# A two-block transformer kernel: the feed-forward's up projection with its units on the partitions

## The chip, the cores and the metric

One core of a Trainium2 chip runs the whole program. The metric is the device time of one execution in microseconds. The kernel before takes 1305.74 us (median of 3 runs, 1304.75 to 1306.25). Engines: PE is TensorE, with PEld its loads of stationary operands; DVE is VectorE, ACT is ScalarE, POOL is GpSimd; SP issues most loads.

## What is computed

256 tokens with 1024 channels pass through a first block (a layer with three kinds of attention and a layer with dilated attention, each followed by a feed-forward) and a second block (feed-forward, a mixer of three branches, feed-forward). The change touches the four feed-forwards alone. They are all of this form, with 2816 hidden units:

```python
def rmsnorm(x, g):
    y = x32 * lax.rsqrt(jnp.mean(x32 * x32, axis=-1, keepdims=True) + RMS_EPS)
    return (y * g.astype(jnp.float32)).astype(x.dtype)

def swiglu(h, w_up, w_down):
    a, b = jnp.split(h @ w_up, 2, axis=-1)
    return (jax.nn.silu(a) * b) @ w_down

x = x + swiglu(rmsnorm(x, norm_ffn[layer]), ffn_w_up[layer], ffn_w_down[layer])
```

The second block adds half of the feed-forward's result.

## The kernel before

**Products in three parts.** Every float32 operand of a large product is split into an upper part, rounded to fp32r, and a lower part, the rest, also fp32r. A product is then upper x upper, upper x lower and lower x upper (`mm3`, L193 to 197). Weights arrive from memory in units of 128 x 2048 numbers, three slots in turn: SP loads a unit into `RAW`, ACT copies it to `WH` (`split_hi`), DVE writes the rest to `WL` (`split_lo`). `hi_done`, `lo_done` and `unit_used` count these.

**A feed-forward stage** (`ffn_sync`, `ffn_scalar`, `ffn_vector`, `ffn_tensor`, r = 0 to 3) takes the 2816 hidden units in 11 steps of 256. A step has an `up` of two weight units (each 4 of the 8 channel blocks, 256 gate columns and 256 value columns) and a `down` of one. In `up`, the tokens are the stationary operand: for each of 2 tiles of 128 tokens and each of 8 channel blocks, `mm3` makes three products of 512 columns (256 gate, 256 value) into the tile's bank, 48 in all. The tile's row scale (the rmsnorm's) is not in the operand; it goes in as the scale of the tanh (`RH`), silu(a) being a(1 + tanh(a/2))/2, and as a factor of the residual (`RF`). For each tile ACT makes the tanh from the bank (L579, L581), DVE two operations (L627, L630), and the gated rows `GG` have tokens on the partitions. PE turns them with four transposes (`turn`, L702) into bank 2, ACT copies the turned rows to `OTH` (L585), DVE writes the rest to `OTL` (L635), and these are the stationary operands of `down`: 24 products of 512 columns into banks 4 to 7, which add up over the 11 steps.

**Order of the work.** Each engine has a list written out by hand, synchronised by counting semaphores. PE: `up(0)`, then in each step `up(s + 2)`, `down(s + 1)`, `turn(s + 2)` (a hardware loop of 8 steps), and at the end `up(10)`, half of `down(9)`, `turn(10)`, the rest of `down(9)`, `down(10)`. In the third stage (r = 2), the memory rows of the mixer are transposed among these last parts (`norm_tensor`).

**The start of a stage.** The stage's input rows are turned tile by tile: `tile_tensor` (L400) has 8 transposes per tile, ACT makes the upper parts (L409), DVE the lower ones (L457, `tile_lo`, counted one by one). Tile 1 is turned in the middle of `up(0)`. `tile_vector` places the split of the second unit between tile 1's fourth and fifth lower part. With `first=True`, `up_half` takes tile 0's upper rows first (L204), its lower rows (L211), turns tile 1, and does the same for it; then comes the second unit, tile by tile (L195 to 197).

## Time and profile before

| | |
|---|---|
| median of 3 runs | 1305.74 us (1304.75 to 1306.25) |
| the profiled execution | 1304.92 us, span from first to last instruction 1303.1 us |
| PE busy | 1270.1 us, 97% |
| PEld busy | 1059.4 us, 81% |
| DVE busy | 811.3 us, 62% |
| ACT busy | 644.9 us, 49% |
| POOL busy | 271.3 us, 21% |
| mean granted clock of PE | 0.996 |
| one transpose of 128 columns (L400), its own length | 272 ns |
| one load of a 128x128 fp32r operand | 188 ns |

The page gives busy time by engine, a strip of 40 slices, the chain of waits that ended last, and groups of instructions. PE is at nine tenths or more in nearly every slice. A product's own duration is longer than the distance to the next one, since they are pipelined; the distances have to be read from start times in the timeline. Times in the rows count from the start of the span.

### The profile page before, as it was taken

To read this page: it belongs to the slowest core of one execution; us is meant where nothing else is said; L and a number is where in the kernel's file an instruction comes from. 1 tells how busy PE (TensorE), PEld (TensorE's weight loads), DVE (VectorE), ACT (ScalarE), POOL (GpSimd) and SP (SyncE) were. 2 spreads that over 40 slices of the span, in tenths; PEclk is the share of its full clock that TensorE was granted. 3 is DMA by queue.
4 is the path that set the end of the run, shared out by engine and by line. 5 is a ranking of instruction groups with operands and counts; after the bars stand their busy time and mean duration, and the time that the engine had idled before them with its cause. 6 is when DMAs were issued, how large, how long until landed. Compare 5 with 4: busy or idle time off the path is not lost.

```text
span 1303.1 us, 19302 instructions
## 1 busy us (share of the span) xinstructions
PE 1270.1 (97%) x7279; PEld 1059.4 (81%) x7279; DVE 811.3 (62%) x1210; ACT 644.9 (49%) x946; POOL 271.3 (21%) x362
## 2 busy tenths in 40 slices
PE   6999999999999999999999999999999999999997
PEld 5986788888799977888888788888887778888886
DVE  3468675555574486654555755556789877755554
ACT  4438654444453366543444655445444683544442
POOL 6420210000000041102000489701186210200000
PEclk9999999999999999999999999999999999999999
DMA  9970556555455644467655465654544436556651
GB/s 288 273 136 19 166 173 193 182 184 186 159 194 180 177 115 130 161 195 175 228 183 179 167 194 186 220 188 147 194 130 146 146 121 202 181 190 193 191 188 41
DMA packets 155883, 224.77 MB, mean 172 GB/s; under 512 B 13395, under 2 KB 107979, under 8 KB 155820
## 3 DMA queue, kind: packets, MB, share of 16 engines
q1 hardware_dynamic: 141008, 208.36, 50.9%
q0 software_dynamic: 10064, 10.54, 4.3%
q10 hardware_dynamic: 4748, 5.02, 1.1%
q8 instruction: 41, 0.67, 0.2%
q14 instruction: 22, 0.18, 0.0%
HBM read 222.56 MB, written 1.25 MB: 172 GB/s over the span
## 4 chain that ended last, share of the span: by engine, by line
PE 80%; DVE 8%; ACT 4%; DMA 4%; issue 2%; POOL 1%; SPq 0%; DVEq 0%; ACTq 0%; POOLq 0%
PE bank L195 23%; PE bank L197 23%; PE bank L196 23%; PE bank L216 4%; DMA raw_units<-in_a_w_in 3%; DVE units_lo L178 3%; PE bank L204 2%; PE bank L702 1%; DMA raw_units<-in_ffn_w_up 1%; ACT arena L1497 1%; DVE arena L2907 1%; PE bank L211 1%; PE bank L1774 1%; DVE arena L2898 1%; ACT units_hi L170 1%
## 5 line engine op out<-in xcount | busy, mean ns | idle before, releaser
L621 DVE TENSOR_TENSOR units_lo<-raw_units,units_hi 128x2048 fp32r<-128x2048 f32 x96 | 223.1, 2324 | 154.2 <-ACT units_hi L575 154.2
L195 PE MATMUL bank<-units_hi,turned_hi 128*128 128x512 f32 (+1 forms) x792 | 307.0, 388 | 3.1 <-DVE units_lo L178 1.3
L197 PE MATMUL bank<-units_hi,turned_lo 128*128 128x512 f32 (+1 forms) x792 | 302.1, 381 | 0.0
L196 PE MATMUL bank<-units_lo,turned_hi 128*128 128x512 f32 (+1 forms) x792 | 301.7, 381 | 0.0
L178 DVE TENSOR_TENSOR units_lo<-raw_units,units_hi 128x2048 fp32r<-128x2048 f32 (+2 forms) x103 | 232.4, 2265 | 109.3 <-ACT units_hi L170 109.1
L170 ACT ACTIVATE units_hi<-raw_units 128x2048 fp32r<-128x2048 f32 (+2 forms) x103 | 193.2, 1886 | 113.3 <-PE bank L197 83.1
L575 ACT ACTIVATE units_hi<-raw_units 128x2048 fp32r<-128x2048 f32 x96 | 183.5, 1911 | 104.0 <-PE bank L197 95.6
L195 PE MATMUL bank<-units_hi,second_hi 128*128 128x512 f32 (+1 forms) x560 | 219.2, 391 | 0.0
L197 PE MATMUL bank<-units_hi,second_lo 128*128 128x512 f32 (+1 forms) x560 | 216.8, 387 | 0.0
L196 PE MATMUL bank<-units_lo,second_hi 128*128 128x512 f32 (+1 forms) x560 | 216.6, 387 | 0.0
L195 PEld LDWEIGHTS bank<-units_hi,turned_hi 128*128 128x128 f32 x792 | 149.0, 188 | 32.8 <-DVE units_lo L178 3.0
L197 PEld LDWEIGHTS bank<-units_hi,turned_lo 128*128 128x128 f32 x792 | 148.9, 188 | 29.2
L196 PEld LDWEIGHTS bank<-units_lo,turned_hi 128*128 128x128 f32 x792 | 149.2, 188 | 26.9
L195 PEld LDWEIGHTS bank<-units_hi,second_hi 128*128 128x128 f32 x560 | 105.4, 188 | 23.4 <-issue 1.7
L197 PEld LDWEIGHTS bank<-units_hi,second_lo 128*128 128x128 f32 x560 | 105.3, 188 | 21.6
L196 PEld LDWEIGHTS bank<-units_lo,second_hi 128*128 128x128 f32 x560 | 105.6, 189 | 20.5
L585 ACT ACTIVATE second_hi<-bank 128x512 fp32r<-128x512 f32 x44 | 26.3, 599 | 127.6 <-PE bank L702 127.6
L261 POOL TENSOR_SCALAR means<-sums 128x1 f32<-128x1 f32 x6 | 2.1, 357 | 363.4 <-ACT rows L249 363.4
L627 DVE SCALAR_TENSOR_TENSOR rows<-rows,bank 128x256 f32<-128x256 f32 x88 | 36.9, 419 | 57.3 <-ACT rows L581 42.0
L635 DVE TENSOR_TENSOR second_lo<-bank,second_hi 128x512 fp32r<-128x512 f32 x44 | 30.4, 690 | 66.6 <-ACT second_hi L585 66.6
L195 PE MATMUL bank<-second_hi,units_hi 128*128 128x256 f32 x240 | 68.3, 285 | 0.0
L196 PE MATMUL bank<-second_lo,units_hi 128*128 128x256 f32 x240 | 67.9, 283 | 0.0
(352 smaller groups left out, 1789.8 us busy)
## 6 DMA issues: line engine op xcount, KB each, us to landing
raw_units<-in_ffn_w_up SPq DMA_DIRECT2D x88, 512.0 KB, 4.8
raw_units<-in_ffn_w_in SPq DMA_DIRECT2D x88, 512.0 KB, 4.6
raw_units<-in_ffn_w_down SPq DMA_DIRECT2D x22, 1024.0 KB, 4.9
raw_units<-in_ffn_w_out SPq DMA_DIRECT2D x22, 1024.0 KB, 4.9
raw_units<-in_w_in SPq DMA_DIRECT2D x18, 1024.0 KB, 5.0
raw_units<-in_b_w_q SPq DMA_DIRECT2D x12, 1024.0 KB, 5.2
raw_units<-in_a_w_in SPq DMA_DIRECT2D x10, 1024.0 KB, 10.7
raw_units<-in_kv_w SPq DMA_DIRECT2D x6, 1024.0 KB, 5.2
```

Source lines behind the costliest of these rows:

```text
L170: act.activation(hi, raw, ACT.Copy).then_inc(m.hi_done, 1)
L178: dve.tensor_tensor(lo, raw, hi.bitcast(F32), ALU.subtract).then_inc(m.lo_done, 1)
L195: pe.matmul(out, lh, rh, start=start, stop=False, skip_group_check=True)
L196: pe.matmul(out, lh, rl, start=False, stop=False, skip_group_check=True)
L197: return pe.matmul(out, ll, rh, start=False, stop=True, skip_group_check=True)
L204: ins = pe.matmul(out, *((rows_hi, w) if stationary else (w, rows_hi)), start=start and x == 0, stop=False, skip_group_check=True)
L216: return pe.matmul(out, lhsT, rhs, start=start, stop=stop, skip_group_check=True)
L575: act.activation(m.WH[:, slot(n0 + j), :], m.RAW[:, slot(n0 + j), :], ACT.Copy).then_inc(m.hi_done, 1)
L585: act.activation(turned(m.OTH, s), m.pb[TR_BANK][:, :], ACT.Copy).then_inc(hi, 1)
L621: dve.tensor_tensor(m.WL[:, slot(n0 + j), :], m.RAW[:, slot(n0 + j), :], m.WH[:, slot(n0 + j), :].bitcast(F32), ALU.subtract).then_inc(m.l ...
L627: dve.scalar_tensor_tensor(out=m.UU[:, t, :], in0=m.TH[:, t, :], scalar=1.0, in1=m.pb[t][:, 0:FSTEP], op0=ALU.add, op1=ALU.mult).then_inc( ...
L635: dve.tensor_tensor(turned(m.OTL, s), m.pb[TR_BANK][:, :], turned(m.OTH, s).bitcast(F32), ALU.subtract)\
```

## The change

In every feed-forward, `up` now has the weights as the stationary operand and the tokens as the moving one, so its result has the hidden units on the partitions, and the gated rows need no turn. Upper and lower rows of the tokens lie side by side in one tile (`HT`), so that one product of 512 columns makes upper weights x (upper rows, lower rows), and a second one of 256 columns adds lower weights x upper rows. Per step that is 2 (`f`, blocks of 128 units) x 2 (`g`, gate or value) x 8 channel blocks x 2. The banks 0 to 3 then hold two halves of 256 columns that belong together: ACT copies the second (`low_tile`, L594), DVE adds the first (`sum_tile`, L658). The row scale now runs along the columns; it is spread over the partitions once per stage, by two products of a matrix of ones with a diagonal one (`FULL`, `DIAG`), and multiplied in by DVE (L663) ahead of the tanh.

The first step is written out apart (`first_step`): the first 128 units' half 0 in products of 128 columns, tile by tile, with tile 1 turned between; then, once all lower rows are there, the rest.

```diff
-    def gate(s, n):
-        act.wait_ge(up_done, s + 1 + f0)
-        act.activation(m.TH[:, 0, :], m.pb[0][:, 0:FSTEP], ACT.Tanh, scale=m.RH[:, 0:1]).then_inc(th, 1)
-        act.wait_ge(m.unit_used, n)
-        act.activation(m.TH[:, 1, :], m.pb[1][:, 0:FSTEP], ACT.Tanh, scale=m.RH[:, 1:2]).then_inc(th, 1)
-
-    def turned_hi(s):
-        act.wait_ge(tr, s + 1 + f0)
-        act.activation(turned(m.OTH, s), m.pb[TR_BANK][:, :], ACT.Copy).then_inc(hi, 1)
+    def low_tile(s, f, used=None):
+
+        if f == 0:
+            act.wait_ge(up_done, s + 1 + f0)
+        else:
+            act.wait_ge(m.unit_used, used)
+        act.wait_ge(lo, s + f0)
+        for dst, bank in ((m.GS, m.pb[2 * f]), (m.US, m.pb[2 * f + 1])):
+            ins = act.activation(dst[:, f, :], bank[:, S:2 * S], ACT.Copy)
+        ins.then_inc(low, 1)
+
+    def low_step(s, used):
+        low_tile(s, 0)
+        low_tile(s, 1, used)
+
+    def gate(s):
+        act.wait_ge(gates, MARKS * (s + f0) + SCALED)
+        act.activation(m.TH, m.TH, ACT.Tanh).then_inc(th, 1)
+
+    def gated_hi(s, used):
+        act.wait_ge(gates, MARKS * (s + f0) + GATED)
+        act.wait_ge(m.unit_used, used)
+        act.activation(gated(m.OTH, s), m.US, ACT.Copy).then_inc(hi, 1)
...
-    turned_hi(NSTEP - 2)
+    gated_hi(NSTEP - 2, n0 + 29)
     split_hi(act, m, n0 + 31)
     if r == 2:
         memory_squares_scalar(act, m)
-    gate(NSTEP - 1, n0 + 31)
     split_hi(act, m, n0 + 32)
-    turned_hi(LAST)
+    low_step(NSTEP - 1, n0 + 31)
+    gate(NSTEP - 1)
+    gated_hi(LAST, n0 + 31)
...
+    def sum_tile(s, f):
+
+        dve.wait_ge(low, 2 * s + f + 1 + 2 * f0)
+        for dst, bank in ((m.GS, m.pb[2 * f]), (m.US, m.pb[2 * f + 1])):
+            ins = dve.tensor_tensor(dst[:, f, :], bank[:, 0:S], dst[:, f, :], ALU.add)
+        ins.then_inc(sums, 1)
+
+    def scale(s):
+        dve.wait_ge(sums, 2 * s + 2 + 2 * f0)
+        dve.tensor_tensor(m.TH, m.GS, m.SPREAD.unsqueeze(1).to_broadcast([P, 2, S]), ALU.mult).then_inc(gates, 1)
+
     def gate(s):
-        for t in range(TT):
-            dve.wait_ge(th, 2 * s + t + 1 + 2 * f0)
-            dve.scalar_tensor_tensor(out=m.UU[:, t, :], in0=m.TH[:, t, :], scalar=1.0,
-                                     in1=m.pb[t][:, 0:FSTEP], op0=ALU.add, op1=ALU.mult).then_inc(u, 1)
-            dve.wait_ge(u, 2 * s + t + 1 + 2 * f0)
-            dve.tensor_tensor(m.GG[:, t, :], m.UU[:, t, :], m.pb[t][:, FSTEP:2 * FSTEP], ALU.mult)\
-                .then_inc(g, 1)
-
-    def turned_lo(s):
+        dve.wait_ge(th, s + 1 + f0)
+        dve.scalar_tensor_tensor(out=m.GS, in0=m.TH, scalar=1.0, in1=m.GS, op0=ALU.add, op1=ALU.mult).then_inc(gates, 1)
+        dve.wait_ge(gates, MARKS * (s + f0) + GATED - 1)
+        dve.tensor_tensor(m.US, m.GS, m.US, ALU.mult).then_inc(gates, 1)
+
+    def gated_lo(s):
         dve.wait_ge(hi, s + 1 + f0)
-        dve.tensor_tensor(turned(m.OTL, s), m.pb[TR_BANK][:, :], turned(m.OTH, s).bitcast(F32), ALU.subtract)\
-            .then_inc(lo, 1)
+        dve.tensor_tensor(gated(m.OTL, s), m.US, gated(m.OTH, s).bitcast(F32), ALU.subtract).then_inc(lo, 1)
+
+    def sum_step(s):
+        sum_tile(s, 0)
+        sum_tile(s, 1)
+        scale(s)
...
+    dve.wait_ge(m.s("tile_scale"), 3 * r + 1)
+    sum_tile(0, 0)
+    dve.memset(m.FULL, 1.0)
+    for t in range(TT):
+        ins = dve.tensor_scalar(m.DIAG[:, t * P:(t + 1) * P], m.IDENT[:, :], m.RH[:, t:t + 1], None, ALU.mult)
+    ins.then_inc(spread, 1)
+    split_lo(dve, m, n0 + 3)
+    sum_tile(0, 1)
+    dve.wait_ge(spread, 3 * r + 3)
+    scale(0)
...
+    def up_products(f, sl, half):
+
+        for g in range(2):
+            bank = m.pb[2 * f + g]
+            for k in range(4):
+                kt, at = 4 * half + k, slice(k * 512 + g * FSTEP + f * P, k * 512 + g * FSTEP + (f + 1) * P)
+                pe.matmul(bank[:, :], m.WH[:, sl, at], m.HT[:, kt].rearrange("p x t -> p (x t)"), start=kt == 0,
+                          stop=False, skip_group_check=True)
+                ins = pe.matmul(bank[:, 0:S], m.WL[:, sl, at], m.HTH[:, kt, :], start=False, stop=kt == KT - 1,
+                                skip_group_check=True)
+        return ins
+
+    def up_half(s, j, e, half):
 
         pe.wait_ge(m.lo_done, n0 + j + half + 1 + e)
...
+        for f in range(2):
+            if half == 0:
+                pe.wait_ge(sums, 2 * s + f - 1 + 2 * f0)
+            ins = up_products(f, slot(n0 + j + half), half)
+            if half == 1 and f == 0:
                 ins.then_inc(up_done, 1)
         ins.then_inc(m.unit_used, 1)
 
...
+    def first_tile(t, x):
+
+        tok = slice(t * P, (t + 1) * P)
+        for k in range(4):
+            if x == 0:
+                pe.wait_ge(m.s("tile_hi"), 8 * r + 4 * t + k // 2 + 1)
+            else:
+                pe.wait_ge(m.s("tile_lo"), 16 * r + 8 * t + k + 1)
+            for g in range(2):
+                at = slice(k * 512 + g * FSTEP, k * 512 + g * FSTEP + P)
+                for w in (m.WH, m.WL)[:2 - x]:
+                    pe.matmul(m.pb[g][:, tok], w[:, slot(n0), at], (m.HTH, m.HTL)[x][:, k, tok],
+                              start=(t, x, k) == (0, 0, 0) and w is m.WH, stop=False, skip_group_check=True)
+
+    def first_step():
+        pe.wait_ge(m.lo_done, n0 + 1)
+        first_tile(0, 0)
+        first_tile(0, 1)
+        tile_tensor(pe, m, r, 1)
+        first_tile(1, 0)
+        first_tile(1, 1)
+        pe.wait_ge(m.lo_done, n0 + 2)
+        pe.wait_ge(m.s("tile_lo"), 16 * r + 16)
+        up_products(0, slot(n0 + 1), 1).then_inc(up_done, 1)
+        up_products(1, slot(n0), 0).then_inc(m.unit_used, 1)
+        up_products(1, slot(n0 + 1), 1).then_inc(m.unit_used, 1)
+        pe.wait_ge(spread, 3 * r + 1)
+        for t in range(TT):
+            tok = slice(t * P, (t + 1) * P)
+            ins = mm(pe, m.pb[7][:, tok], m.FULL, m.DIAG[:, tok], t == 0)
+        ins.then_inc(spread, 1)
...
-    up(0, 0, 0, first=True)
-    up_half(1, 2, 0, 0, free=0)
-    turn(0)
-    up_half(1, 2, 0, 1)
+    def up(s, j, e):
+        for half in range(2):
+            up_half(s, j, e, half)
+
+    first_step()
+    up(1, 2, 0)
     down(0, 4, 0, True)
-    turn(1)
     with pe.Fori(0, NSTEP - 3) as s:
         up(s + 2, 5, 3 * s)
         down(s + 1, 7, 3 * s, False)
-        turn(s + 2)
     up(LAST, 29, 0)
     down(NSTEP - 2, 31, 0, False, (0,))
-    turn(LAST)
     if r == 2:
-        norm_tensor(pe, m, 5, m.C.MEM, banks=(0, 1, 2))
+        pe.wait_ge(sums, 2 * NSTEP + 2 * f0)
+        norm_tensor(pe, m, 5, m.C.MEM)
     down(NSTEP - 2, 31, 0, False, (1,))
-    if r == 2:
-        pe.wait_ge(lo, NSTEP + f0)
-        norm_tensor(pe, m, 5, m.C.MEM, banks=(3,))
     down(LAST, 32, 0, False)
...
-    m.HTH, m.HTL = sb("turned_hi", [P, KT, S], F32R), sb("turned_lo", [P, KT, S], F32R)
+    m.HT = sb("turned", [P, KT, 2, S], F32R)
+    m.HTH, m.HTL = m.HT[:, :, 0, :], m.HT[:, :, 1, :]
...
-    m.TH = cut.take(TT, FSTEP)
-    m.UU = cut.take(TT, FSTEP)
-    m.GG = cut.take(TT, FSTEP)
+    m.GS = cut.take(2, S)
+    m.US = cut.take(2, S)
+    m.TH = cut.take(2, S)
+    m.SPREAD = cut.take(S)
+    m.DIAG, m.FULL = cut.take(S), m.TH[:, 0, 0:P]
```

**PE in the loop, at the end of a step.** The last three products of a `down` (banks 6 and 7), and what followed them before; bank 2 takes the turned rows, `rows` are the gated ones:

```order
L195 MATMUL bank7<-units_hi,second_hi 128x512
L196 MATMUL bank7<-units_lo,second_hi 128x512
L197 MATMUL bank7<-units_hi,second_lo 128x512
L699 ISA
L702 MATMUL bank2<-ident,rows 128x128 [waits ffn_gated]
L702 MATMUL bank2<-ident,rows 128x128 x3
L734 REGISTER_ALU
L734 COMPARE_AND_BRANCH
L195 MATMUL bank0<-units_hi,turned_hi 128x512 [waits lo_done]
L196 MATMUL bank0<-units_lo,turned_hi 128x512
L197 MATMUL bank0<-units_hi,turned_lo 128x512
```

Now the next step's `up` follows at once, with the weights (`units_hi`, `units_lo`) as the stationary operand and the tokens (`turned`) moving, 512 and 256 columns in turn:

```order
L195 MATMUL bank7<-units_hi,second_hi 128x512
L196 MATMUL bank7<-units_lo,second_hi 128x512
L197 MATMUL bank7<-units_hi,second_lo 128x512
L803 REGISTER_ALU
L803 COMPARE_AND_BRANCH
L725 MATMUL bank0<-turned,units_hi 128x512 [waits ffn_sums,lo_done]
L727 MATMUL bank0<-turned,units_lo 128x256
L725 MATMUL bank0<-turned,units_hi 128x512
L727 MATMUL bank0<-turned,units_lo 128x256
```

The rows of the turn and its wait are gone; the wait on the gated rows is replaced by one on the sums, which free bank 0.

**PE in the first step of a stage.** The end of tile 1's part and the second unit, before; the wait on `tile_lo` (the lower rows, counted one by one) stands at each channel block:

```order
L204 MATMUL bank1<-units_hi,turned_hi 128x512 [waits tile_hi]
L204 MATMUL bank1<-units_lo,turned_hi 128x512
L211 MATMUL bank1<-units_hi,turned_lo 128x512 [waits tile_lo] x4
L195 MATMUL bank0<-units_hi,turned_hi 128x512 [waits tile_lo,lo_done]
L196 MATMUL bank0<-units_lo,turned_hi 128x512
L197 MATMUL bank0<-units_hi,turned_lo 128x512
L195 MATMUL bank0<-units_hi,turned_hi 128x512 [waits tile_lo]
L196 MATMUL bank0<-units_lo,turned_hi 128x512
L197 MATMUL bank0<-units_hi,turned_lo 128x512
L195 MATMUL bank0<-units_hi,turned_hi 128x512 [waits tile_lo]
```

The same place now:

```order
L753 MATMUL bank0<-turned,units_hi 128x128 [waits tile_lo]
L753 MATMUL bank1<-turned,units_hi 128x128
L753 MATMUL bank0<-turned,units_hi 128x128 [waits tile_lo]
L753 MATMUL bank1<-turned,units_hi 128x128
L725 MATMUL bank0<-turned,units_hi 128x512 [waits tile_lo,lo_done]
L727 MATMUL bank0<-turned,units_lo 128x256
L725 MATMUL bank0<-turned,units_hi 128x512
L727 MATMUL bank0<-turned,units_lo 128x256
```

And the end of the first step, with the two products of the row scales, ahead of step 1:

```order
L725 MATMUL bank3<-turned,units_hi 128x512
L727 MATMUL bank3<-turned,units_lo 128x256
L216 MATMUL bank7<-rows 128x128 [waits ffn_spread]
L216 MATMUL bank7<-rows 128x128
L725 MATMUL bank0<-turned,units_hi 128x512 [waits ffn_sums,lo_done]
L727 MATMUL bank0<-turned,units_lo 128x256
```

The second unit's products, which took the lower rows as they came, tile 0 first, now stand behind one wait for all sixteen of them.

## Rows read from the trace of the kernel before

**Rows 1.** The chain that ended last, shares of the span by engine and by line

```profile
PE 80%; DVE 8%; ACT 4%; DMA 4%; issue 2%; POOL 1%; SPq 0%; DVEq 0%; ACTq 0%; POOLq 0%
PE bank L195 23%; PE bank L197 23%; PE bank L196 23%; PE bank L216 4%; DMA raw_units<-in_a_w_in 3%; DVE units_lo L178 3%; PE bank L204 2%; PE bank L702 1%; DMA raw_units<-in_ffn_w_up 1%; ACT arena L1497 1%; DVE arena L2907 1%; PE bank L211 1%; PE bank L1774 1%; DVE arena L2898 1%; ACT units_hi L170 1%
```

**Rows 2.** Timeline of PE, two turns of gated rows one loop step apart

```profile
558.05 0.60 PE L702 MATMUL bank<-ident,rows 128*128 128x128 f32 x4
...
574.85 0.60 PE L702 MATMUL bank<-ident,rows 128*128 128x128 f32 x4
```

**Rows 3.** Timeline of PE, 512-column products in a row, 32 pitches apart (same columns)

```profile
204.63 0.39 PE L197 MATMUL bank<-units_hi,turned_lo 128*128 128x512 f32 x1
...
211.88 0.39 PE L196 MATMUL bank<-units_lo,second_hi 128*128 128x512 f32 x1
```

**Rows 4.** Timeline of PE, 256-column products in a row, 68 pitches apart

```profile
403.79 0.28 PE L197 MATMUL bank<-second_hi,units_lo 128*128 128x256 f32 x1
...
411.95 0.28 PE L196 MATMUL bank<-second_lo,units_hi 128*128 128x256 f32 x1
```

**Rows 5.** Timeline of PE, full 128x128 stationary operands, few moving columns

```profile
80.54 3.66 PE L216 MATMUL bank<-arena 128*128 128x32 f32 x32
...
87.42 1.90 PE L216 MATMUL bank<-arena,rows 128*128 128x64 f32 x16
...
165.07 1.03 PE L400 MATMUL bank<-ident,residual 128*128 128x128 f32 x8
```

**Rows 6.** Timeline of PE, first step of the first feed-forward

```profile
166.64 0.39 PE L204 MATMUL bank<-units_hi,turned_hi 128*128 128x512 f32 x1
...
169.38 1.03 PE L400 MATMUL bank<-ident,residual 128*128 128x128 f32 x8
...
173.83 0.50 PE L195 MATMUL bank<-units_hi,turned_hi 128*128 128x512 f32 x1 [0.34 <-DVE units_lo L178]
...
179.41 0.39 PE L195 MATMUL bank<-units_hi,turned_hi 128*128 128x512 f32 x1
```

**Rows 7.** Timeline of ACT, then of DVE, the same stretch

```profile
169.79 2.18 ACT L409 ACTIVATE turned_hi<-bank,gain_cols 128x128 fp32r<-128x128 f32 x8 [1.09 <-PE bank L400]
...
170.45 1.13 DVE L457 SCALAR_TENSOR_TENSOR turned_lo<-bank,gain_cols,turned_hi 128x128 fp32r<-128x128 f32 x4 [1.55 <-ACT turned_hi L409]
...
171.50 2.28 DVE L178 TENSOR_TENSOR units_lo<-raw_units,units_hi 128x2048 fp32r<-128x2048 f32 x1
...
173.69 1.12 DVE L457 SCALAR_TENSOR_TENSOR turned_lo<-bank,gain_cols,turned_hi 128x128 fp32r<-128x128 f32 x4
```

**Rows 8.** Timelines of DVE, POOL and PE, first step of the third feed-forward

```profile
725.23 1.12 DVE L457 SCALAR_TENSOR_TENSOR turned_lo<-bank,gain_cols,turned_hi 128x128 fp32r<-128x128 f32 x4
...
730.01 0.25 POOL L486 TENSOR_SCALAR gate_scales<-rsqrts 128x2 f32<-128x2 f32 x1
...
731.82 0.47 PE L195 MATMUL bank<-units_hi,turned_hi 128*128 128x512 f32 x1 [0.72 <-DVE rows L630]
```

**Rows 9.** Timelines of PE, ACT and DVE: durations for the last step

```profile
342.00 0.39 PE L195 MATMUL bank<-units_hi,second_hi 128*128 128x512 f32 x1
...
342.20 0.47 ACT L581 ACTIVATE rows<-bank,gate_scales 128x256 f32<-128x256 f32 x1 [2.25 <-PE bank L197]
...
345.36 0.60 ACT L585 ACTIVATE second_hi<-bank 128x512 fp32r<-128x512 f32 x1 [0.88 <-PE bank L702]
...
357.15 3.03 ACT L295 ACTIVATE turned_hi<-bank,gain_cols 128x256 fp32r<-128x256 f32 x8 [2.08 <-PE bank L346]
...
358.02 3.23 DVE L327 SCALAR_TENSOR_TENSOR turned_lo<-bank,gain_cols,turned_hi 128x256 fp32r<-128x256 f32 x8 [1.01 <-ACT turned_hi L295]
...
714.16 0.69 DVE L505 TENSOR_TENSOR rows<-residual,arena 128x512 f32<-128x512 f32 x1
```

**Rows 10.** Windows inside the third block (us, each engine's busy time, granted clock)

```profile
1007.00:1010.50 3.50, 1.28 (x11) 0.80 (x12) 3.33 (x16) 1.91 (x1) 3.26 (x4) 1.00 0.69 220
1010.50:1014.00 3.50, 3.50 (x13) 1.92 (x12) 3.50 (x6) 0.00 (x0) 0.00 (x0) 0.51 0.23 84
```

More of the change, by code:

```diff
@@ L33 @@
 ULEN = 2048
[L34 removed]
+DOWN_BANK = 4
 MASKED, TAKEN = -3.0e38, -3.3e38
@@ L557, with gated, gated_columns @@
 LAST = NSTEP - 1
-def turned(tiles, s):
+MARKS, SCALED, GATED = 3, 1, 3
+def gated(tiles, s):
     k = 2 if s is LAST else 0
-    return tiles[:, k:k + 2, :].rearrange("p k t -> p (k t)")
+    return tiles[:, k:k + 2, :]
+def gated_columns(tiles, s):
+    return gated(tiles, s).rearrange("p k t -> p (k t)")
 def ffn_scalar(act, m, r):
     n0, f0 = first_unit(f"ffn{r}"), r * NSTEP
-    up_done, th, tr, hi = (m.s(f"ffn_{x}") for x in ("up0", "tanh", "transposed", "hi"))
+    up_done, low, gates, th, hi, lo, spread = (
+        m.s(f"ffn_{x}") for x in ("up0", "low", "gates", "tanh", "hi", "lo", "spread"))
     def split(j, s):
@@ L655, in ffn_vector @@
         memory_scale_vector(dve, m)
+    split_lo(dve, m, n0 + 32)
+    sum_step(NSTEP - 1)
     gate(NSTEP - 1)
[L657 to L658 removed]
+    gated_lo(LAST)
 def ffn_tensor(pe, m, r, following=None):
     n0, f0 = first_unit(f"ffn{r}"), r * NSTEP
[L663 to L690 removed]
@@ new lines, in ffn_tensor @@
+    up_done, sums, lo, spread = (m.s(f"ffn_{x}") for x in ("up0", "sums", "lo", "spread"))
+    def up_products(f, sl, half):
[8 more added lines that the diff above has]
+        return ins
```

69 lines of the change are left out of this document (19 added, 50 removed).

## The prediction

> **What bounds the kernel now.** I read the chain of waits first. PE is 80% of it, and the three products of `mm3` (L195 to L197) are 69% [rows 1]: products that follow each other without a gap, while the other engines work beside them. So the sum goes by PE's start-to-start pitches and by the places where PE has to wait; what DVE and ACT gain or lose matters only at those. An instruction's own duration (0.39 us for 512 columns) overlaps the next and is no price. The views give these pitches. In a run of 512-column products 32 pitches take 211.88 - 204.63 = 7.25 us, 0.2267 us each [rows 3]. With 256 columns 68 pitches take 8.16 us, 0.120 us each [rows 4]. The line through both is 0.4167 ns a column plus 13.3 ns a product. A step of the loop takes 574.85 - 558.05 = 16.80 us [rows 2]; its 72 products of 512 columns take 72 x 0.2267 = 16.32, so the turn (four transposes and the change to and from them) costs 0.48 us of PE.
>
> **Turns removed.** 4 stages x 11 turns x 0.48 = **-21.2 us**. All of it is on the path, since PE has no gap around a turn.
>
> **Up products.** A step had 48 products of 512 columns; it now has 32 of 512 and 32 of 256. The columns are the same 24,576, but there are 16 products more, each with a stationary operand of its own: 32 x 0.2267 + 32 x 0.120 - 48 x 0.2267 = +0.213 us. For steps 1 to 10 of four stages that is 40 x 0.213 = **+8.5 us**. No row has 512 and 256 columns in turn. The bounds are 0 and twice this value; I take the line, because each product in both streams has its own load, as here, and the 13.3 ns is there at either length.
> The Trainium skill, page TensorE: Matmul & The Clock Gate, section "Wait — 56ns, not 53.3ns?", gives a fixed 2.5 ns per matmul beyond its columns. By that the 640 more products would cost 1.6 us instead of 8.5. The trace has 13.3 ns where every product has a load, so the sum does not use it.
>
> **First step.** This is where PE gets a new wait. Before, PE did tile 0's products, turned tile 1, did tile 1's upper rows, and went on with half 1 of tile 0 (173.83) while tile 1's last lower rows were still being made; step 1 began at 179.41 [rows 6]. Now both groups of units beyond the first 128-column one wait for all 16 lower-row parts. In the first stage: tile 0's 24 products have 128 columns. At 0.108 us each they take 2.6 us against 169.38 - 166.64 = 2.74 [rows 6], so tile 1 is turned about 0.14 earlier. The chain behind that is not shortened: ACT makes the upper rows from 169.79, DVE four lower parts from 170.45, then the 2.28 us split of unit 1, which stands ahead of the last four parts in DVE's queue, and these end at 173.69 + 1.12 = 174.81 [rows 7]; now 174.67. PE has done tile 1's 24 short products by about 173.0 and idles 1.7 us. Then come three groups of eight 512 and eight 256 products, 3 x 8 x (0.2267 + 0.120) = 8.3 us, and the two products that spread the row scales, estimated at 0.6 us with the change of kind, restart 0.1. Step 1 starts at 183.75 instead of 179.41: +4.3. The second and fourth stages have the same order of work: +4.3 each. In the third, PE's wait of 0.72 us for the gate, which came from POOL's scale at 730.01, goes away [rows 8]; its last lower part ends at 725.23 + 1.12 = 726.35 as before, so step 1 starts at 726.35 + 9.0 = 735.3 instead of 731.82: +3.4. Together **+16.3 us**.
> The price of a 128-column product with such operands has no row. Bounds: 0.067 us by the line above, 0.227 us if it costs as much as one of 512 columns. The nearest rows are full 128x128 stationary operands with 32, 64 and 128 columns: (3.66 - 0.27)/31, (1.90 - 0.27)/15 and (1.03 - 0.27)/7 all give 0.108 to 0.109 us [rows 5] (0.27 being one product's own length), whatever the columns; so a change of such an operand has a floor there, and I take 0.108. At 0.067, three stages gain 1.1 us each, -3.2 in all. The spread's bounds are 0.2 and 0.9 us a stage.
>
> **Last step.** The gated rows of step 10 used to be turned in the middle of a `down` of step 9. Now a chain of nine operations has to fit beside that `down`: from its start (342.00), ACT can begin after 0.20 us [rows 9]; two copies of 256 columns 0.84 (eight took 3.03); two sums on DVE 0.81 (eight of the same size took 3.23); the product with the spread scale 0.69; tanh 0.60; the gate's two operations 2 x 0.69; the upper copy 0.60; the lower part 0.69; and eight hand-overs, estimated at 0.04. That is 6.1 us, with the restart 6.2, against a cover of 24 x 0.2267 = 5.44: PE waits 0.8 us. The third stage has 16 transposes of the memory rows there as further cover and waits not at all. 3 x 0.8 = **+2.4 us**, between 0 (the copies and sums pipeline better) and 4.5.
>
> **At no cost.** In the other steps the same chain starts at the end of `up` and its result is needed 16 us later; the sums, which free the banks for the next `up`, come after some 2 us under a `down` of 5.44. DVE's work per step becomes 3 x 2.28 + 2 x 0.81 + 4 x 0.69 = 11.2 us, below the 16.5 of PE, and ACT, with shorter splits and fewer operations, stays below DVE. If that cover were gone, a step would grow by what they exceed it. DVE now waits for POOL's scale ahead of its first sum; behind it stands the split of unit 3, which is needed 5.5 us into step 1, and the scale is there at 730.3, 5 us before that step. SP's loads are the same, and no queue is moved past another.
>
> **Sum.** -21.2 + 8.5 + 16.3 + 2.4 = +6.0 us on the profiled execution's 1304.92 (span 1303.1), so 1310.9; the median of the runs lies 0.8 higher, at 1305.74, which gives **1311.7**. This case alone spans 1308.5 to 1315. About 0.2%, 2.6 us, is what a measurement can tell from no change.
>
> **Rivals.**
> 1. *Short products are dear.* If 128 columns cost 0.227 us, tile 0's work takes 5.4 us instead of 2.7, tile 1 is turned 2.7 later, and its own 24 products end near 178.6: step 1 starts at some 187.6, +8.2 in each stage. 1311.7 + 4 x 8.2 - 16.3 = 1328. For it: all fp32r products in the trace have 256 columns or more, so their price below is unseen. Against it: the floor of 0.108 at every width [rows 5]. Chance 0.22.
> 2. *No change.* 0.067 us per short product (-3.2) and a last chain that fits under `down` (-2.4): 1306.1. For it: PE's idle 1.7 us is bounded by DVE and shrinks only if tile 1 comes earlier, which this does. Against it: both must be kind. Chance 0.17.
> 3. *640 more products cost nearly nothing.* With 2.5 ns instead of 13.3 for each, 1311.7 - 6.9 = 1304.8, no change. This is what the page's rule above gives. The measured pitches speak against it [rows 3, 4]. Chance 0.04.
> 4. *Faster.* The change of operand hides behind the pairs of long and short products on the same bank. Then +8.5 becomes 0, the first step's 24 x 4 pairs give back 1.3, and the short products take 0.067 (-3.2): 1311.7 - 13.0 = 1298.7. Its place is the up products of every step. It turns the sign where an added product costs less than 3.9 ns: the other terms make -21.2 + 16.3 + 2.4 = -2.5 us, and 640 x 3.9 ns = 2.5. Against it: 13.3 ns shows in both uniform streams. Chance 0.08.
> A granted clock that falls belongs to the upper end: a stretch with PE busy 1.28 of 3.5 us was followed by one at 0.51, the level of 1.2 GHz [rows 10]. The new idle of 1.7 us is shorter than the 2.2 there, so I count nothing; if it fell ahead of the dense products, 3.4 us at half speed cost 1.7 us a stage, 6.8 at most.
>
> **Numbers.** Forecast 0.49, rivals 0.22, 0.17, 0.04 and 0.08. Faster: rival 4, 0.08. Within 0.2%: rivals 2 and 3 with a little of the forecast, 0.23. Slower: 0.69. The range runs from 1304.5 (rivals 3 and 2 within) to 1329 (rival 1 within); rival 4 and a remainder are left out.
>
> **What would show it.** Loop steps of 16.53 us instead of 16.80; pairs of products that take 0.347 us; PE waiting for the lower rows near 173 to 174.7 in the first stage and step 1 starting 4.3 us later; a wait of about 0.8 us ahead of the last `down` in three stages, none in the third; no transposes from gated rows. I am wrong if pairs take clearly less than 0.347 (rival 4) or 128 columns near 0.227 (rival 1), or if PE waits inside the loop.

## The result, and the profile after

The changed kernel takes **1330.8 us** (median of 4 runs, 1328.2 to 1331.9), the kernel before 1305.7 on the same chip: a ratio of 1.0182, 95% interval 1.0170 to 1.0195. It is slower, as forecast, but by 25 us where the forecast had 6, and outside the range. The profiled run took 1330.84 us. Times below are medians of a kernel's runs; only one run was slow (4178.8 us, of the kernel without turns), and it is left out. The kernel before, measured again beside each, took 1305.7 to 1307.1 us.

The engines' busy time and the chain that ended last (before: [rows 1]):

```profile
span 1328.6 us, 21186 instructions
PE 1289.7 (97%) x7951; PEld 1098.7 (83%) x7951; DVE 903.8 (68%) x1354; ACT 692.3 (52%) x1082; POOL 278.3 (21%) x362
PE bank L725 24%; PE bank L727 12%; PE bank L195 12%; PE bank L197 11%; PE bank L196 11%; PE bank L216 5%; DVE units_lo L178 3%; DMA raw_units<-in_a_w_in 2%; PE bank L204 1%; ACT arena L1562 1%; DVE arena L2972 1%; PE bank L1839 1%; DVE arena L2963 1%; DVE turned L457 1%; ACT units_hi L170 1%
```

PE is as full as before, so the 25.5 us of span are in how long its products take and in a few gaps. Three places hold them. First the loop: PE's timeline, start of an `up`, its first pair (a product of 512 columns and the one of 256 behind it), start of the `down` behind it, start of the next `up`:

```profile
205.09 0.39 PE L725 MATMUL bank<-turned,units_hi 128*128 128x512 f32 x1
205.32 0.28 PE L727 MATMUL bank<-turned,units_lo 128*128 128x256 f32 x1
205.43 0.40 PE L725 MATMUL bank<-turned,units_hi 128*128 128x512 f32 x1
...
216.38 0.40 PE L195 MATMUL bank<-units_hi,second_hi 128*128 128x512 f32 x1
...
221.89 0.39 PE L725 MATMUL bank<-turned,units_hi 128*128 128x512 f32 x1
```

The `up` takes 216.38 - 205.09 = 11.29 us, 0.3528 a pair, the `down` 5.51, the step 16.80: exactly as before [rows 2], where 16.53 was forecast. All `up`s in the loops take 11.29 but the one below. Step 1, ahead of the loop, has the same 64 products in the same order, and there an `up` takes 11.38 in the first and fourth stage and 11.18 in the second and third:

```profile
557.06 0.47 PE L725 MATMUL bank<-turned,units_hi 128*128 128x512 f32 x1
...
568.24 0.39 PE L195 MATMUL bank<-units_hi,second_hi 128*128 128x512 f32 x1
```

In the slower one the pairs follow each other at 0.350, 0.361 and 0.349 us in turn, in the quicker one at 0.350 and 0.343, which is the forecast's 0.347. In the five profiled kernels that keep this `up` unedited, 10 of 20 executions of step 1 are quick and 10 slow. So the order alone does not set the price; what decides between the two is not shown. Then the first step (before: [rows 6]):

```profile
169.64 0.22 PE L753 MATMUL bank<-turned,units_hi 128*128 128x128 f32 x1
169.70 0.27 PE L753 MATMUL bank<-turned,units_lo 128*128 128x128 f32 x1
...
171.26 0.27 PE L753 MATMUL bank<-turned,units_lo 128*128 128x128 f32 x1
...
177.88 0.47 PE L725 MATMUL bank<-turned,units_hi 128*128 128x512 f32 x1 [1.60 <-DVE turned L457]
...
187.85 0.61 PE L216 MATMUL bank<-rows 128*128 128x128 f32 x4
188.21 0.48 PE L725 MATMUL bank<-turned,units_hi 128*128 128x512 f32 x1
```

Products of 128 columns start 0.111 us apart: 14 pitches in 171.26 - 169.70 = 1.56. PE waits 1.60 us for DVE, and the 24 pairs behind that take 187.85 - 177.88 = 9.97 us where 8.3 was forecast. The windows around it say why (us, PE's busy time, granted clock, DMA share, GB/s):

```profile
173.00:176.50 3.50, 3.22 (x28) 1.00 0.00 0
176.50:180.00 3.50, 2.12 (x8) 0.77 0.58 151
180.00:183.50 3.50, 3.50 (x17) 0.75 0.92 307
```

The last two share one stretch at 0.5, the level of 1.2 GHz: 3.5 x (0.23 + 0.25) = 1.7 us lost, so 3.4 us long. The first step takes 18.57 us (12.77 before) in the first and second stage, 19.43 (14.33) in the third, which had such a stretch too, 17.01 (12.78) in the fourth, which had none: +20.9 us. Third, one `up` of the third stage (from 852.68) takes 13.18 us instead of 11.29. DVE and POOL there:

```profile
850.70 1.61 DVE L667 SCALAR_TENSOR_TENSOR rows<-rows 128x512 f32<-128x512 f32 x1 [0.70 <-ACT rows L603]
851.84 2.73 POOL L2881 TENSOR_TENSOR arena<-arena 128x1024 f32<-128x1024 f32 x1
852.35 2.77 DVE L669 TENSOR_TENSOR rows<-rows 128x512 f32<-128x512 f32 x1
855.04 3.98 DVE L651 TENSOR_TENSOR units_lo<-raw_units,units_hi 128x2048 fp32r<-128x2048 f32 x1
...
859.07 0.50 PE L725 MATMUL bank<-turned,units_hi 128*128 128x512 f32 x1 [0.59 <-DVE units_lo L651]
```

L669 takes 0.69 elsewhere; here it ends 0.55 us after the POOL operation that had begun before it. The rest of the span: three waits ahead of the last `down` (below), 1.1 us; and stretches at half clock outside the stages, near 86, 366 and 1032 us, against near 17 and 1011 before.

### The profile page after: what moved, and what is told of

It reads as the page before. It is cut to its first block, busy times and chain, and to the rows that moved or that the text cites. A ratio compares the mean times of both kernels' runs of the same rounds, so it can differ in the third digit from the quotient of the medians.

```text
span 1328.6 us, 21186 instructions
## 1 busy us (share of the span) xinstructions
PE 1289.7 (97%) x7951; PEld 1098.7 (83%) x7951; DVE 903.8 (68%) x1354; ACT 692.3 (52%) x1082; POOL 278.3 (21%) x362
## 4 chain that ended last, share of the span: by engine, by line
PE 81%; DVE 9%; ACT 4%; issue 2%; DMA 2%; POOL 2%; DVEq 0%; SPq 0%; ACTq 0%; POOLq 0%
PE bank L725 24%; PE bank L727 12%; PE bank L195 12%; PE bank L197 11%; PE bank L196 11%; PE bank L216 5%; DVE units_lo L178 3%; DMA raw_units<-in_a_w_in 2%; PE bank L204 1%; ACT arena L1562 1%; DVE arena L2972 1%; PE bank L1839 1%; DVE arena L2963 1%; DVE turned L457 1%; ACT units_hi L170 1%
## 5 line engine op out<-in xcount | busy, mean ns | idle before, releaser
L725 PE MATMUL bank<-turned,units_hi 128*128 128x512 f32 x1376 | 491.9, 401 | 7.0 <-DVE turned L457 6.4
L727 PE MATMUL bank<-turned,units_lo 128*128 128x256 f32 x1376 | 388.1, 282 | 0.0
L725 PEld LDWEIGHTS bank<-turned,units_hi 128*128 128x128 f32 x1376 | 260.7, 189 | 71.6 <-issue 6.8
L651 DVE TENSOR_TENSOR units_lo<-raw_units,units_hi 128x2048 fp32r<-128x2048 f32 x96 | 226.1, 2358 | 106.3 <-ACT units_hi L584 106.3
L727 PEld LDWEIGHTS bank<-turned,units_lo 128*128 128x128 f32 x1376 | 262.0, 190 | 1.4
L594 ACT ACTIVATE rows<-bank 128x256 f32<-128x256 f32 x176 | 58.0, 382 | 139.8 <-PE bank L727 135.0
L658 DVE TENSOR_TENSOR rows<-bank,rows 128x256 f32<-128x256 f32 x176 | 66.0, 418 | 61.3 <-ACT rows L594 61.3
L197 PE MATMUL bank<-second_hi,units_lo 128*128 128x256 f32 x240 | 67.9, 283 | 0.0
L603 ACT ACTIVATE rows<-rows 128x512 f32<-128x512 f32 x44 | 27.8, 632 | 76.5 <-DVE rows L663 76.5
L216 PE MATMUL bank<-arena 64*64 64x64 f32 (+6 forms) x804 | 66.5, 304 | 0.0
```

Source lines behind the costliest of these rows:

```text
L197: return pe.matmul(out, ll, rh, start=False, stop=True, skip_group_check=True)
L216: return pe.matmul(out, lhsT, rhs, start=start, stop=stop, skip_group_check=True)
L594: ins = act.activation(dst[:, f, :], bank[:, S:2 * S], ACT.Copy)
L651: dve.tensor_tensor(m.WL[:, slot(n0 + j), :], m.RAW[:, slot(n0 + j), :], m.WH[:, slot(n0 + j), :].bitcast(F32), ALU.subtract).then_inc(m.l ...
L658: ins = dve.tensor_tensor(dst[:, f, :], bank[:, 0:S], dst[:, f, :], ALU.add)
L725: pe.matmul(bank[:, :], m.WH[:, sl, at], m.HT[:, kt].rearrange("p x t -> p (x t)"), start=kt == 0, stop=False, skip_group_check=True)
```

## The experiments

All kernels but one are built on the changed one. A step's `up` and `down` are read off PE's timeline as above. The line is the prediction's, through the two uniform streams: it gives 11.09 us for an `up`.

**Products in groups of four.** In `up_products`:

```diff
-            for k in range(4):
-                pe.matmul(bank[:, :], m.WH[:, sl, at], m.HT[:, kt]...)
-                ins = pe.matmul(bank[:, 0:S], m.WL[:, sl, at], m.HTH[:, kt, :]...)
+            for w in (m.WH, m.WL):
+                for k in range(4):
...
```

> Edit: in each group of eight pairs' worth of up products on one bank, the four products of 512 columns come first and the four of 256 behind them, instead of in turn. Nothing else changes. Theory A (a change of length after every product costs more than the line through the uniform streams says: 0.3528 us a pair against 0.347, and 0.06 us over the first products of the down behind it): with an eighth as many changes an up falls from 11.29 us towards 11.1, a down from 5.50 towards 5.45, a loop step from 16.80 to about 16.55, and 40 steps give about -10 us: 1321. Theory B (the extra price belongs to each 256-column product with a load of its own, whatever stands around it): up stays within 0.03 us of 11.29 and the time within 0.1% of 1330.8. The first steps keep their idle time and their clock either way.

Measured 1324.0 us, ratio 1.0132 (1.0109 to 1.0155). An `up` takes 11.20, a `down` 5.49: a step of 16.69, half way, which fits neither theory's number. Two of the four first steps had their half clock instead of three.

**A uniform stream of 256 columns.**

```diff
-                pe.matmul(bank[:, :], m.WH[:, sl, at], m.HT[:, kt]...)
+                pe.matmul(bank[:, 0:S], m.WH[:, sl, at], m.HTH[:, kt, :]...)
+                pe.matmul(bank[:, S:2 * S], m.WH[:, sl, at], m.HTL[:, kt, :]...)
```

> Edit: each up product of 512 columns (upper and lower rows side by side) is split into two of 256 on the two halves of the bank, so that a step's up is 96 products of 256 columns, the same 24,576 columns in a uniform stream, and 32 more products than in the changed kernel. Theory A (13.3 ns for each product with a load, the line of the prediction, holds in a uniform stream; the alternation costs extra): 96 x 0.120 = 11.52 us an up and 5.45 a down, so a loop step of 16.97, +0.17 against 16.80, and with the first steps' three groups (24 x 3 x 0.120 = 8.64 instead of 8.4) about +8 us: 1339. Theory C (an added product costs 2.5 ns, as the Trainium skill, page TensorE: Matmul & The Clock Gate, gives it): up is at most 11.0, and the time falls by some 10 us. Theory B (the price belongs to the short product, 0.126 instead of 0.120 wherever it stands in an up): 96 x 0.126 = 12.1 us an up and 1362.

Measured 1336.5 us (1.0208 to 1.0247). Its `up`, from one start to the `down`:

```profile
220.70 0.28 PE L725 MATMUL bank<-turned,units_hi 128*128 128x256 f32 x1
...
232.21 0.40 PE L195 MATMUL bank<-units_hi,second_hi 128*128 128x512 f32 x1
...
237.68 0.28 PE L725 MATMUL bank<-turned,units_hi 128*128 128x256 f32 x1
```

11.51 us for 96 products, 0.1199 each, and a step of 16.98: theory A to the hundredth (its time of 1339 was 2.5 us too high). So an added product costs 13.3 ns in this kernel, and what the changed kernel pays above that comes from mixing the lengths. The Trainium skill, page TensorE: Matmul & The Clock Gate, section "Wait — 56ns, not 53.3ns?", has 2.5 ns; these fp32r streams, each product with its own load, do not show it.

**The first step reordered.** DVE splits unit 1 after the last lower parts, PE does the group that needs unit 0 alone first:

```diff
     tile_lo_vector(dve, m, r, 1, range(0, 4))
-    split_lo(dve, m, n0 + 1)
     tile_lo_vector(dve, m, r, 1, range(4, KT))
+    split_lo(dve, m, n0 + 1)
...
-        pe.wait_ge(m.lo_done, n0 + 2)
         pe.wait_ge(m.s("tile_lo"), 16 * r + 16)
-        up_products(0, slot(n0 + 1), 1).then_inc(up_done, 1)
         up_products(1, slot(n0), 0).then_inc(m.unit_used, 1)
+        pe.wait_ge(m.lo_done, n0 + 2)
+        up_products(0, slot(n0 + 1), 1).then_inc(up_done, 1)
```

> Edit: in the first step DVE makes the last four lower-row parts ahead of the lower part of weight unit 1, and PE does the group of half 0 for the second 128 units (which needs unit 0 alone) ahead of the two groups that need unit 1. The same products are made. Theory A (the first step's +20.9 us over four stages are an idle time of 1.6 us that comes from DVE's queue, and behind it in three stages a stretch at half clock, 1.6 us each; the rest is work): the idle falls from 1.6 us to under 0.3, the granted clock behind it stays at 1, and step 1 starts 3.2 us earlier in the first and second stage, up to 3.2 in the third, 1.6 in the fourth: about -11 us, 1320. Theory D (the clock falls because of the short products, not of the idle time): the idle goes, the clock stays at 0.5 for 3.4 us: about -6 us, 1325. Theory E (the chain behind it, copies of the first sums and the splits of units 2 and 3, is what holds step 1): step 1 starts within 0.5 us of now.

Measured 1317.4 us, ratio 1.0076 (1.0056 to 1.0096), 13.4 us less than the changed kernel.

```profile
174.15 0.61 PE L753 MATMUL bank<-turned,units_hi 128*128 128x128 f32 x4
174.60 0.45 PE L725 MATMUL bank<-turned,units_hi 128*128 128x512 f32 x1
...
183.49 0.47 PE L725 MATMUL bank<-turned,units_hi 128*128 128x512 f32 x1
```

No wait here (0.33 us are left in the third stage); the pairs take 8.53 us. The first steps are 3.20, 3.20, 2.74 and 1.63 us shorter, 10.8 in all: theory A. The other 2.6 us lie outside what was edited: the first stage begins 1.5 us earlier, and the stretch at half clock near 366 us is not there.

**The wait filled.** Ahead of the two waits:

```diff
+        for x in range(7):
+            pe.matmul(m.pb[4][:, :], m.WH[:, slot(n0), 0:P], m.HT[:, 0]...)
```

> Edit: the wait for the lower rows stays as it is, but PE fills the 1.6 us before it with seven more products of 512 columns into a bank that nobody reads (7 x 0.2267 = 1.59 us). This work is not part of the computation. Theory A (the stretch at half clock in three of the four first steps follows from the idle time): the granted clock stays at 1 there, the 24 pairs take 8.4 us instead of 10.0, and step 1 starts 1.6 us earlier in three stages: about -4.8 us, 1326. Theory D (the short products or something else lower the clock): unchanged or slightly slower, 1331 to 1332.

Measured 1323.9 us (1.0107 to 1.0149), 6.9 less, 4.3 of it in the first steps (1.4, 1.4, 1.5, 0). The windows of the first stage are at full clock:

```profile
172.00:175.50 3.50, 3.50 (x26) 1.00 0.00 0
175.50:179.00 3.50, 3.50 (x21) 1.00 0.91 291
179.00:182.50 3.50, 3.50 (x23) 1.00 0.90 289
```

So the idle time is needed for the clock to fall here: with the same short products and without it, the clock stayed up. No first step has this idle time without short products ahead of it, so whether it would be enough by itself is not shown. Work that nobody reads, put into the idle time, makes the kernel faster. The rest of the 6.9 is outside the stages, where stretches at half clock come and go between runs.

**Longer groups.** The loop over `w` is put outside both `f` and `g` in half 0, outside `g` in half 1.

> Edit: still fewer changes of length. In half 0 of an up all 16 products of 512 columns come first, then all 16 of 256; in half 1 eight and eight for each 128 units: 6 changes an up, where the grouped kernel had 16 (up 11.20 us) and the changed one 64 (11.29). Theory A (each change of length costs; the line without changes gives 32 x 0.2267 + 32 x 0.120 = 11.09): up falls to 11.13, a loop step from 16.69 to about 16.6, some -3 us against the grouped kernel's 1324, so 1321, less 1.6 for each first step that escapes the half clock. Theory B (the remaining 0.11 us of the grouped kernel has nothing to do with changes): up stays at 11.20 and the time within 2 us of 1324.

Measured 1326.1 us (1.0123 to 1.0161): `up` 11.13, `down` 5.47, a step of 16.60, theory A's number. The time did not follow: with its waits for free banks moved forward, the `up` of step 1 takes 11.5 to 12.1 and that beside POOL's tables 14.26; and three first steps were at half clock, against two in the grouped kernel.

**The kernel before without its turns.**

```diff
-        for q in range(2):
-            for t in range(TT):
-                ins = pe.transpose(m.pb[TR_BANK]..., m.GG[:, t, q * P:(q + 1) * P], m.IDENT[:, :])
-        ins.then_inc(tr, 1)
```

> Built on the kernel before. Edit: the four transposes of each turn are left out; ACT waits for the gated rows itself and copies whatever lies in the bank. The turned gated rows are thus not computed, all else is. Theory A (the first term of the prediction, 0.48 us of PE for each of 44 turns): loop steps of 16.32 to 16.34 us instead of 16.80 and 1284.6. Then the changed kernel's step of 16.79 means that its up and the beginning of its down cost 0.47 us more than before, against 0.213 in the prediction. Rival (a part of the 0.48 is the change from one kind of product to the next, or a wait that stays): steps of 16.45 or more, 1290 or more; then the up products' price was right and the removed term was too large.

Measured 1288.1 us (ratio 0.9836 to 0.9875), 18.6 less: between theory A's 1284.6 and the rival's 1290, so the steps have to decide. Two `down`s, one step apart:

```profile
209.91 0.39 PE L195 MATMUL bank<-units_hi,second_hi 128*128 128x512 f32 x1
...
226.23 0.39 PE L195 MATMUL bank<-units_hi,second_hi 128*128 128x512 f32 x1
```

16.32 us: theory A; a turn in the loop is worth its 0.48, and the changed step of 16.80 costs 0.48 more than this one. The first stage, from its first product to the transposes behind it, takes 352.96 - 169.94 = 183.0 us where it took 188.1, 5.1 less, against 11 x 0.48 = 5.3 by the term. It begins 3.3 us later than before [rows 6], outside all that was edited, which covers the 2.6 us missing from 21.2.

**POOL's last doubling left out.** `while n < S // 2` for `while n < S` in the tables of the third stage; the second half of each table row is not computed.

> Built on the changed kernel. Edit: in the third stage POOL leaves out the last doubling of its tables, six operations of 128x1024 (1.90 to 3.83 us each) and five small ones; the second half of each table row is thus not computed. Theory F (the up of 13.18 us in the third stage, 1.89 above the others, comes from DVE's operations of SBUF to SBUF, which take 1.6 to 2.8 us instead of 0.69 beside these POOL operations): that up takes 11.29 to 11.5 us, DVE's gate operations there stay below 1.2 us, and the time is 1.5 to 1.9 us shorter. Rival (the table load of 1.28 us on ACT in that step, or the weights' DMA, is what delays it): the up keeps 12.5 us or more.

Measured 1327.6 us (1.0135 to 1.0176); the `up` in question takes 11.29: theory F, though one of DVE's gate operations still took 1.69 us, beside POOL's doubling before that. The time says little, since one first step had two stretches at half clock in a row (11.33 us for its pairs).

**Both repairs.**

> Edit: both repairs on the changed kernel, the reordered first step (13.4 us by itself) and the longer groups. If they are independent, the time is that of the reordered start, 1317.4, less what the longer groups give in a loop step times 40: 1310 by theory A (step 16.6), 1313 by theory B (step 16.69). No stretch at half clock in any first step. Neither reaches the kernel before (1305.7), since the 48 products of 128 columns (5.3 us a stage where 24 pairs would be 2.8) and the steps' price remain.

Measured 1314.9 us (1.0042 to 1.0080). Steps of 16.60, no half clock in a first step, but step 1's `up` takes 12.0, since it comes earlier to a bank that DVE's sums have not freed (a wait of 0.45 us <-DVE L658 in the first stage). That makes 4 x 0.8 us, and the `up` beside POOL's tables is 1.1 longer than in the changed kernel, 14.26: most of the 5 us by which theory A's 1310 was missed. The two repairs are not independent.

**The first step made from rows.** Step 0 as in the kernel before (L204, L211, four transposes into bank 6), step 1 beginning with `f = 1`, and each `f` and half grouped eight and eight. PE's list (ACT's and DVE's follow it):

```diff
-    first_step()
-    up(1, 2, 0)
+    rows_half(0)
+    rows_half(1)
+    up_half(1, 2, 0, 0)
+    first_turn()
+    up_half(1, 2, 0, 1)
```

> Edit on the changed kernel: step 0 of each stage is made as in the kernel before (rows stationary, its gated rows turned by four transposes, one turn a stage instead of eleven), step 1 begins with the second 128 units, whose banks are free, and the up products of each 128 units and half are grouped, eight of 512 columns and then eight of 256. Theory A (what the change costs sits in the 128-column products and the wait of its first step, and in the changes of length of its ups): from the start of a stage to the end of step 0 as before (12.8 us, 14.3 in the third stage), step 1 longer by a turn and the spread products (0.8 us), loop steps of 16.60 to 16.63 against 16.80 before: 40 x -0.18 = -7.2, plus 1.4 for the spreads, 1.1 for three waits ahead of the last down, 2 to 3 for the step beside POOL's tables: 1306.7 - 2 = 1304, within 0.3% of the kernel before and some 25 us below the changed one. Rival (the columns made from rows and the ones made from units hinder each other in step 1, whose gate has a cover of 2.8 us only): PE waits there over 0.5 us a stage and the time is 1307 or more.

Measured 1304.8 us, ratio 0.9989 (0.9974 to 1.0003). The first step takes 12.77, 12.77, 13.50 and 12.80, a loop step 16.62, step 1 12.03 against 11.35 before; no wait there. Theory A. The interval includes 1, so this kernel is not shown to be faster than the kernel before.

> The changed kernel, unedited, beside the kernel above on one chip: it tells how often its first steps have the stretch at half clock. Theory A (each such stretch costs 1.6 us and comes after the idle time in most, not all, stages; others of 1.7 us elsewhere come and go in every kernel): 1328 to 1332 us, spread over about 4 us, with two to four of the four first steps at 10.0 us for their 24 pairs and the rest at 8.4 to 8.5.

Measured 1331.1 us (1326.3 to 1333.5), ratio 1.0187. All four first steps had the stretch (9.99, 9.91, 11.32, 10.09), and so all in all 26 of the 32 first steps of the eight profiled kernels that keep the wait, and none of the 12 of the three that fill or avoid it.

**Groups of two.**

> Built on the changed kernel, for the price of a change of length alone. Edit: two products of 512 columns, then two of 256, in turn: 32 changes an up. An up of 32 + 32 products is 11.09 us by the line; it took 11.13 with 6 changes (7 ns each above the line), 11.20 with 16 (7 ns each) and 11.29 with 64 (3 ns each). Theory A (each change costs 7 ns as long as products of one length stand at least two together, and less in strict turn): 11.30 to 11.32 us. Theory B (the price lies between, 4 to 5 ns each): 11.22 to 11.26. Either way the time stays within 0.5% of the changed kernel's 1330, and its first steps as they are.

Measured 1321.6 us (1.0092 to 1.0150).

```profile
219.96 0.39 PE L729 MATMUL bank<-turned,units_hi 128*128 128x512 f32 x1
...
231.09 0.40 PE L195 MATMUL bank<-units_hi,second_hi 128*128 128x512 f32 x1
...
236.54 0.39 PE L729 MATMUL bank<-turned,units_hi 128*128 128x512 f32 x1
```

11.13 and 5.45: with 32 changes as cheap as with 6, cheaper than with 16. A price per change is refuted, and so are both my theories. This kernel also bears on POOL's tables: their six operations of 128x1024 follow each other as in the changed kernel, with DVE's list unedited, and yet no `up` of the third stage takes over 11.14 us.

```profile
843.93 2.31 POOL L2884 TENSOR_TENSOR arena<-arena 128x1024 f32<-128x1024 f32 x1
...
845.44 0.39 PE L729 MATMUL bank<-turned,units_hi 128*128 128x512 f32 x1
...
856.57 0.40 PE L195 MATMUL bank<-units_hi,second_hi 128*128 128x512 f32 x1
```

Here the first of them begins as DVE's L669 does (843.8); in the changed kernel it began 1.3 us ahead of DVE's L663 (847.56 against 848.86). That is the difference between the two that the traces show; so it seems to count where in DVE's step they fall, which no run tests by itself.

**The other bank.** In turn, but a short product never behind a long one on its own bank.

> Built on the changed kernel. Edit: long and short products stay in turn (28 of 32 changes a half), but the short one behind a long one goes to the other bank of the two (order: long to bank 0, short to bank 1, long to bank 1, short to bank 0). Theory G (the price of strict turn is the short product's accumulation onto the bank and columns that the long product just before it is writing): up falls from 11.29 to 11.10 to 11.15, the down behind it to 5.45, and the time by 9 to 10 us. Theory H (the price comes from the lengths in turn, whatever the bank, for instance because each long product's weights have to be loaded beside a short one): up stays at 11.27 or more.

Measured 1327.2 us (1.0129 to 1.0164). `up` 11.27, `down` 5.46: for the `up` theory H, the bank is not the cause of its price. The `down` came out as theory G had it; but the last two products ahead of it are now both short, so the bank and the order are not told apart there.

**POOL's wide operations apart.** On the kernel with the first step from rows, in the tables' last doubling, first with x = 3, 4, 5, then with 4, 5, 6:

```diff
+        turn = lambda x: pool.wait_ge(m.lo_done, first_unit("ffn2") + 9 + 3 * x) if n == S // 2 else None
+        turn(4)
         link(pool.tensor_tensor(t0, c0, wc, ALU.mult))
         link(pool.tensor_tensor(t1, s0, ws, ALU.mult))
+        turn(5)
...
```

> Edit on the kernel with the first step made from rows: POOL's six operations of 128x1024 in the third stage no longer follow each other, but come two by two, each pair after the second weight split of one of three successive steps. Same work, same numbers. Theory F (the up of 14.26 us there, 3.1 above the others, is DVE's queue, whose SBUF to SBUF operations take up to four times as long beside these six, so that five of them delay a lower weight part): with at most two per step DVE keeps inside its step of 16.6 us (11.2 of work and 4 to 5 of stretch), PE waits under 0.3 us, that up takes 11.2 to 11.5 and the time is 3 us less: 1301.8, faster than the kernel before by 0.3%. Rival (any two of them in the gate chain are enough): one up in each of three steps is 1 us longer and nothing is gained.

Measured 1302.3 us, ratio 0.9968 (0.9956 to 0.9980). Four operations still followed each other, since the count awaited had been reached; that `up` took 13.15 instead of 14.26. The time came out as expected, the mechanism only in part: of the 2.5 us less, 1.1 lie in this `up`, and the rest is luck.

> The kernel with the first step made from rows, with POOL's six wide operations two by two as in e13, but each pair one step later (the counter awaited by the first pair had been reached 4 us before, that by the second had been reached too, so four stood together and the up took 13.15 instead of 14.26 or 11.15). Theory F (PE's wait there is DVE's queue, delayed by more than its slack of 5 us a step only when four or more wide operations fall into one): PE waits under 0.3 us, no up in that stage over 11.5, 1.6 to 2 us less than e13's 1302.25: 1300.5. Rival (two are enough): ups of 12 us or more, time as e13.

Measured **1301.4 us**, ratio 0.9954 (0.9939 to 0.9969): 0.5% less than the kernel before, and faster than both kernels. POOL's pairs now lie in three steps, the last four operations being

```profile
841.65 2.40 POOL L2911 TENSOR_TENSOR arena<-arena 128x1024 f32<-128x1024 f32 x1 [10.00 <-DVE units_lo L657]
844.13 1.90 POOL L2912 TENSOR_TENSOR arena<-arena 128x1024 f32<-128x1024 f32 x1
858.26 1.90 POOL L2914 TENSOR_TENSOR arena<-arena 128x1024 f32<-128x1024 f32 x1 [12.23 <-DVE units_lo L657]
860.23 2.40 POOL L2915 TENSOR_TENSOR arena<-arena 128x1024 f32<-128x1024 f32 x1
```

and no `up` of that stage's loop takes over 11.15 us. The rival is out, since two are not enough here to delay PE. Theory F's cause holds (without POOL's wide operations, or with these spaced, PE's wait is gone), but not its threshold of four: in the groups of two, six in a row brought no wait. The time fell by 0.9 us, not by 1.6 to 2, and its interval overlaps that of the spacing before; the `up` is what shows the gain. Against the kernel with the first step from rows (0.9974 to 1.0003) the intervals are apart.

## Why the prediction was right and wrong

- **Turns, -21.2 us: right.** 16.80 became 16.32 without them, and a stage 5.1 us shorter. (44 x 0.48 is 21.1, and the third stage's first step comes to +3.5, not +3.4: two slips of 0.1.)
- **Up products, +8.5 us: the step that failed.** The line itself holds for uniform streams (0.1199 us, 16.98 a step). What failed is "pairs that take 0.347", a price for the mixed stream taken from uniform ones: in the loops a pair takes 0.3528, and the first `down` products behind it another 0.05. A step pays 0.48, not 0.213: over 40 steps 40 x 0.27 = 10.7 us more, and the loop gained nothing. The bounds, 0 and twice the value, did not reach it, and the signs of being wrong named only pairs that take less. Why strict turn costs 0.20 us over the line and groups of four 0.11, where groups of two, eight and sixteen cost 0.04 to 0.06, stays open, as does why half of the step 1 `up`s run at 0.347 a pair and every loop step at 0.3528.
- **First step, +16.3: the mechanism right, one factor left out.** Short products at 0.111 (0.108 forecast), a wait of 1.60 (1.7), and the fourth stage, alone at full clock, at +4.23 (4.3). Counting nothing for the clock was wrong: the new wait brought the half clock in three of four stages, 1.6 us each, within the 6.8 that the text had as the most. The rows behind it [rows 10] were read as a limit, with an idle time of 2.2 us; 1.6 was enough.
- **Last step, +2.4: the place right, too dear.** The waits were 0.36 us each, and none in the third stage, as foreseen; from ACT's first copy (350.93) to the end of DVE's lower part (356.61) the chain took 5.68 us, where the sum had 5.93, and the `down` that covers it was itself 0.05 longer:

```profile
356.76 0.47 PE L195 MATMUL bank<-units_hi,second_hi 128*128 128x512 f32 x1 [0.36 <-DVE second_lo L673]
```

- **At no cost: wrong in one step of 44.** DVE's sum of 11.2 us a step was right, but [rows 9] has its durations beside an idle POOL. "If that cover were gone, a step would grow": it was gone where POOL's wide operations ran, +1.9 us. The Trainium skill, page SBUF — State Buffer, section "SBUF: two separate sides", says that a DVE operation with two inputs in SBUF and a GpSimd operation that reads SBUF exclude each other for a whole instruction. The trace agrees: 0.69 became 2.77, while operations with one input in a bank kept their length (before: 0.41 to 0.42 in this place). The change turned the second kind into the first.
- **Rival 1**, 1328, hit the total and is false: the short products cost 0.111 us, not 0.227. The total was made of three other errors, 10.7 for the pairs, 4.8 for the clock and 1.9 for POOL, less 1.3 in the last steps: that it hit is luck. That makes 16.1 of the 19.1 us between forecast and result. Another 3.0 us lie ahead of the first stage, which begins that much later than before with the same program there; over the sixteen profiles its start lies between 166.6 and 169.9 us. That is scatter between executions, and no effect of the change is shown in it.

## What to carry to other kernels

Price a mixed stream of products from a mixed stream, or not more surely than the gain it is to bring; two products of each length at a time was as good as any order tried. Ask of a new wait on PE what it does to the clock as well: here 1.6 us idle cost 3.2 where the clock fell, and moving one operation in DVE's queue and one group of products in PE's took both away. An operand moved from a bank to SBUF can bring DVE into POOL's way, at a place far from the change.

## What was not expected of the hardware

- Products of 512 and 256 columns in strict turn: 0.3528 us a pair in every loop step, but either 0.347 or 0.353 in the same order in step 1; 0.348 in groups of two, 0.350 in groups of four.
- A stretch of 3.4 us at the level of 1.2 GHz after 1.6 us of idle time behind 56 products and transposes of 128 columns, in 26 of 32 cases, and in none of 12 without the idle time.
- DVE's 128x512 operations on SBUF: 0.69 us alone, up to 2.77 beside POOL; the weight splits 2.29 and up to 4.48 (DVE, at 861.24).
